# One expert phase of a hybrid encoder layer: rows moved between halves of a turn, a coefficient tile released earlier, and part of a split moved from GpSimd to VectorE

## The reference, cut to what matters

```python
u = jnp.take(u_tab, ib, axis=0)                     # 128 rows of 2048 for each token
h = jax.nn.gelu(jnp.einsum('nkd,nd->nk', u, xb), approximate=False)
vv = jnp.take(v_tab, ib, axis=0)
return jnp.einsum('nk,nkd->nd', gb * h, vv)
```

## Time and profile before

| what | us |
|---|---|
| median of 3 runs | 4788.26 (4786.75 to 4789.27) |
| the profiled execution | 4788.95 |
| its span in the trace | 4787.2 |
| PE busy | 4449.2 (93%) |
| DVE busy | 2972.1 (62%) |
| POOL busy | 2434.3 (51%) |
| ACT busy | 1360.4 (28%) |

### The profile page before, as it was taken

One profiled execution on the slowest core, in us unless ns is written; L12 is line 12 of the kernel. 1 busy time (PEld: TensorE's weight loads), 2 busy tenths in 40 slices (PEclk: granted clock), 3 DMA queues, 4 the chain that ended last, 5 costly groups with the idle time before them and its releaser, 6 DMA issues. The chain is left out here.

```text
span 4787.2 us, 86830 instructions
## 1 busy us (share of the span) xinstructions
PE 4449.2 (93%) x33921; PEld 4303.0 (90%) x33921; DVE 2972.1 (62%) x4301; ACT 1360.4 (28%) x1786; POOL 2434.3 (51%) x929
## 2 busy tenths in 40 slices
PE   6999989999999898979999989999999999999997
PEld 5999888888888798969999989999999999999997
DVE  4333255555555432239996946666787887777786
ACT  3333322222222221122223433332223223233222
POOL 1322222222212133324443347787898998888885
PEclk8999999999999999989999999999999999999998
DMA  6999833444343467853334478888898889888884
GB/s 233 355 360 371 294 126 121 135 136 136 127 136 132 136 221 248 299 196 107 102 114 155 188 270 283 281 286 313 326 333 324 329 322 330 311 306 323 307 297 168
DMA packets 357708, 1141.22 MB, mean 238 GB/s; under 512 B 35089, under 2 KB 128657, under 8 KB 270225
## 3 DMA queue, kind: packets, MB, share of 16 engines
q1 hardware_dynamic: 294400, 780.38, 47.0%
q0 software_dynamic: 46080, 335.56, 18.8%
q10 hardware_dynamic: 17040, 22.58, 1.3%
HBM read 942.00 MB, written 195.32 MB: 238 GB/s over the span
## 5 line engine op out<-in xcount | busy, mean ns | idle before, releaser
L154 POOL TENSOR_TENSOR wlo<-raw,whi 128x2048 fp32r<-128x2048 f32 x174 | 804.1, 4621 | 1981.9 <-ACT whi L150 1686.0
L168 POOL TENSOR_TENSOR wlo<-raw,whi 128x1024 fp32r<-128x1024 f32 x424 | 1067.2, 2526 | 262.0 <-ACT whi L164 258.1
L164 ACT ACTIVATE whi<-raw 128x1024 fp32r<-128x1024 f32 x424 | 448.6, 1059 | 1067.5 <-PE psS L236 553.2
L236 PE MATMUL accs<-xh,whi 128*128 128x272 f32 x2624 | 580.8, 303 | 56.4 <-POOL wlo L154 26.3
L236 PE MATMUL psS<-hh,whi 128*128 128x384 f32 x1600 | 556.2, 348 | 57.1 <-DVE H L2270 52.4
L236 PE MATMUL accs<-xh,wlo 128*128 128x272 f32 x2624 | 546.7, 290 | 0.0
L236 PE MATMUL accs<-xl,whi 128*128 128x272 f32 x2624 | 545.7, 290 | 0.0
L2295 DVE SCALAR_TENSOR_TENSOR H<-R,HD,H 128x2048 f32<-128x2048 f32 x127 | 528.6, 4162 | 0.1
L236 PE MATMUL accs<-hh,whi 128*128 128x272 f32 (+1 forms) x1696 | 459.4, 320 | 49.0 <-POOL wlo L154 24.5
L236 PEld LDWEIGHTS accs<-xh,whi 128*128 128x128 f32 x2624 | 415.9, 190 | 86.9 <-issue 39.3
L236 PE MATMUL psS<-hl,whi 128*128 128x384 f32 x1344 | 465.3, 346 | 0.0
(11 more groups left out here) (424 smaller groups left out, 8973.6 us busy)
## 6 DMA issues: line engine op xcount, KB each, us to landing
raw<-in_u SPq DMA_DIRECT2D x128, 1024.0 KB, 4.9
raw<-in_v SPq DMA_DIRECT2D x128, 1024.0 KB, 5.3
raw<-in_w_in SPq DMA_DIRECT2D x82, 1024.0 KB, 8.1
at_UI<-in_u SPq DMA_DIRECT2D x64, 1024.0 KB, 9.4
u_d<-at_UO SPq DMA_DIRECT2D x256, 256.0 KB, 6.6
wo_UI<-in_u SPq DMA_DIRECT2D x24, 1024.0 KB, 8.9
u_d<-wo_UO SPq DMA_DIRECT2D x96, 256.0 KB, 4.8
g_d<-STG SPq DMA_DIRECT2D x8, 3072.0 KB, 9.7
```

Source lines behind the costliest of these rows:

```text
L154: pool.tensor_tensor(self.lo[:, c % 2, :], self.raw[:, c % 2, :], self.hi[:, c % 2, :].bitcast(F32), ALU.subtract).then_inc(self.split_don ...
L164: act.activation(self.half(self.hi, c, h), self.half(self.raw, c, h), ACT.Copy).then_inc(self.hi_done, 1)
L168: pool.tensor_tensor(self.half(self.lo, c, h), self.half(self.raw, c, h), self.half(self.hi, c, h).bitcast(F32), ALU.subtract).then_inc(se ...
L236: mm = pe.matmul(out, w(k), x(k, n), start=a, stop=z)
```

## The change

It does three things, and adjusts the order around them.

- The rows of a turn: `places` now has 9 of a turn's 13 rows in units 0 to 3. DVE runs `rows(2)`, `rows(2)` at the start of the u half, then as before, so 10 rows stand ahead of the adds of unit 4 and 3 (4 in long turns) in the v half; none stands ahead of unit 7's adds.
- The second half of wlo of each u unit of a turn is made by DVE (`u_second`, semaphore `u_second`), not by POOL. It waits for POOL's first half and for both halves of whi. SP's loads and TensorE's waits for these units go by the two counts (`second_load`, `second_ready`). The one for unit 0 stands between adds 13 and 14 of the turn before, unit 1's after two rows, those of units 2 and 3 after `coef_lo(0)` and `coef_lo(1)`.
- In the first groups, TensorE's first block of the last channel of the last v unit, the last that reads chi and clo tile 0, signals `ex_free`, and ACT makes chi tile 0 on that; tiles 1 to 3 wait as before.

The four loads of H also share one semaphore.

```diff
+        def second_load(sp, src, i, n):
+            if 2 <= n < 6:
+                sp.wait_ge(S["u_second"], 4 * i + n - 1)
+            else:
+                sp.wait_ge(W.split_done, 12 * i + before_u + (2 * n - 2 if n < 2 else 2 * n - 6))
...
+        def second_ready(pe, i, n, half):
+            if n < 4 and half:
+                pe.wait_ge(S["u_second"], 4 * i + n + 1)
+            else:
+                pe.wait_ge(W.split_done, 12 * i + before_u + (n + 1 if n < 4 else 2 * n - 4 + half + 1))
+
+        def u_second(dve, c):
+            dve.wait_ge(W.split_done, 12 * ((c - C0) // U) + before_u + (c - C0) % U + 1)
+            dve.wait_ge(W.hi_done, 2 * (W.base + c) + 2)
+            dve.tensor_tensor(W.half(W.lo, c, 1), W.half(W.raw, c, 1), W.half(W.hi, c, 1).bitcast(F32),
+                              ALU.subtract).then_inc(S["u_second"], 1)
...
-                    W.split_lo_half(pool, c, h)
+                    if c < C0 or (c - C0) % U >= 4 or h == 0:
+                        W.split_lo_half(pool, c, h)
...
-                    done(channel(c, dd, [*range(4)]), dd)
+                    if h == 3 and dd == 3 and per == 4:
+                        channel(c, dd, [0]).then_inc(S["ex_free"], 1)
+                        done(channel(c, dd, [1, 2, 3]), dd)
...
-                        W.wait_used(act, c)
                         for k in range(4):
+                            if k == 0:
+                                act.wait_ge(S["ex_free"], s + 1)
+                            else:
+                                W.wait_used(act, c)
                             coef_hi(4 * s + 4 + k)
...
-                rows(3 if kinds[s] == "long" else 2)
+                c = C0 + U * (s - FIRST)
+                rows(2)
+                u_second(dve, c + 1)
+                rows(2)
                 for k in range(2):
                     scale(4 * s + k)
                     rows(1)
                     coef_lo(4 * s + k)
+                    u_second(dve, c + 2 + k)
                     rows(1)
...
                         if dd == 2:
-                            rows(1)
+                            rows(1 if h == 1 or kinds[s] == "long" else 0)
                         add(s, 4 * h + dd)
-                rows(1)
                 for dd in range(4):
                     add(s, 12 + dd)
+                    if dd == 1:
+                        u_second(dve, c + U)
```

More of the change, by code:

```diff
@@ L1935, in experts @@
                   "last": [(0, 0.1), (0, 0.5), (1, 0.3), (1, 0.7), (2, 0.3), (2, 0.7), (3, 0.3)],
[L1936 to L1939, removed]
+                  "short": [(0, 0.1), (0, 0.4), (0, 0.7), (1, 0.0), (1, 0.3), (1, 0.7), (2, 0.3), (2, 0.6), (3, 0.3),
+                            (4, 0.3), (5, 0.1), (5, 0.7), (6, 0.2)],
+                  "long": [(0, 0.1), (0, 0.4), (0, 0.7), (1, 0.0), (1, 0.3), (1, 0.7), (2, 0.3), (2, 0.6), (3, 0.3),
+                           (4, 0.3), (5, 0.1), (5, 0.7), (6, 0.2), (6, 0.7)]}
         dotted = summed = 0
@@ L1956, in experts @@
         issue = [max(3.0, when[n - GBUF] + 0.4 if n >= GBUF else 0.0) for n in range(len(gathers))]
+        before_u = 2 * (W.base + C0) + 4
+        def second_load(sp, src, i, n):
[3 more added lines that the diff above has]
+                sp.wait_ge(W.split_done, 12 * i + before_u + (2 * n - 2 if n < 2 else 2 * n - 6))
+            raw = W.raw[:, n % 2, :]
+            if len(src.shape) == 3:
+                raw = raw.rearrange("p (k n) -> p k n", k=src.shape[1])
+            sp.dma_start(raw, src).then_inc(W.loaded[n % 2], 16)
+        def second_ready(pe, i, n, half):
[8 more added lines that the diff above has]
+                              ALU.subtract).then_inc(S["u_second"], 1)
         def gates_stored(eng):
@@ L2011, in groups @@
                 for k in range(4):
-                    W.load(sp, row(A["u"], 4 * s + k), C0 + k, U, i)
+                    second_load(sp, row(A["u"], 4 * s + k), i, k)
                 for h in range(4):
-                    v_unit(C0 + 4 + h, i, s, h, U)
+                    src = v_units[s, h] if isinstance(s, int) else v_units[bass.ds(s, 1), h].rearrange("g p k n -> (g p) k n")
+                    second_load(sp, src, i, 4 + h)
                 if not last:
@@ L2058, in u_products @@
                 for h in range(2):
-                    W.ready(pe, c, per, i, h)
+                    if per == U:
+                        second_ready(pe, i, c - C0, h)
+                    else:
+                        W.ready(pe, c, per, i, h)
                     for mm in product(pe, [out], lambda k: W.hi[:, c % 2, k * P:(k + 1) * P], lambda k: W.lo[:, c % 2, k * P:(k + 1) * P],
@@ L2078, in v_first @@
                 for half in range(2):
-                    W.ready(pe, c, per, i, half)
+                    if per == U:
+                        second_ready(pe, i, c - C0, half)
+                    else:
+                        W.ready(pe, c, per, i, half)
                 for k in range(4):
@@ L2096, in v_products @@
                 for dd in range(4):
-                    if dd % 2 == 0:
+                    if dd % 2 == 0 and per == U:
+                        second_ready(pe, i, c - C0, dd // 2)
+                    elif dd % 2 == 0:
                         W.ready(pe, c, per, i, dd // 2)
                     pe.wait_ge(S["ex_added"], 16 * s + 4 * h + dd + 1)
-                    done(channel(c, dd, [*range(4)]), dd)
+                    if h == 3 and dd == 3 and per == 4:
+                        channel(c, dd, [0]).then_inc(S["ex_free"], 1)
+                        done(channel(c, dd, [1, 2, 3]), dd)
+                    else:
+                        done(channel(c, dd, [*range(4)]), dd)
             def v_units_of(c, i, s, per):
@@ L2159, in _ @@
             for q in range(4):
-                act.dma_start(H[:, 4 * q:4 * q + 4, 0:TD], load_h(4 * q, 4 * q + 4)[:, :, 0:TD]).then_inc(S[f"ex_h{q}"], 16)
+                act.dma_start(H[:, 4 * q:4 * q + 4, 0:TD], load_h(4 * q, 4 * q + 4)[:, :, 0:TD]).then_inc(S["ex_h"], 16)
             act.wait_ge(S["ex_cst"], 16)
@@ L2263, in add @@
                 h, dd = d // 4, d % 4
-                if s == 0 and dd == 0:
-                    dve.wait_ge(S[f"ex_h{h}"], 16)
+                if s == 0 and d == 0:
+                    dve.wait_ge(S["ex_h"], 64)
                 if dd % 2:
@@ L2314, in _ @@
                     add(s, 4 * h + 3)
+                    if h == 3 and not ahead:
+                        u_second(dve, C0)
                     if h == 1 and ahead:
@@ L2336, in _ @@
                         if dd == 2:
-                            rows(1)
+                            rows(1 if h == 1 or kinds[s] == "long" else 0)
                         add(s, 4 * h + dd)
-                rows(1)
                 for dd in range(4):
                     add(s, 12 + dd)
+                    if dd == 1:
+                        u_second(dve, c + U)
             s = SUPERS - 1
-            rows(2)
+            c = C0 + U * (s - FIRST)
+            rows(1)
+            u_second(dve, c + 1)
+            rows(1)
             for k in range(3):
@@ L2347, in _ @@
                 coef_lo(4 * s + k)
+                if k < 2:
+                    u_second(dve, c + 2 + k)
                 rows(1 if k < 2 else 0)
```

## The result

The changed kernel takes 4838.1 us (median, 4828.8 to 4840.2) beside 4788.7 for the kernel before: ratio 1.0095, interval 1.0079 to 1.0111. It is slower by 49 us where 76 us less were forecast. Its profiled execution took 4828.82 us (span 4827.0), 39.9 more than the profiled one before.

What follows compares the result with a forecast made beforehand. TensorE was taken as the bound, losing time to waits and clock. Turns 62 + first groups 10.6 + odd turns 5 + 0.5 + 0 - 2 = 76 us less, giving 4712 us; range 4680 to 4775.

Steps and rivals of the forecast that it cites:

- What bounds the kernel, and the floor: Supers 13 to 29: TensorE is the bound; a turn's floor is 67.2 us against 72.9 measured before.
- The rows: Turn's end: with the rows moved, waits of 3.5 and 0.4 us a turn go, and the clock's loss with them.
- some 1 us to spare: End of long turns: despite a second row at unit 6, adds 12 and 13 end in time by this margin.
- `u_second`: DVE's second half of wlo for u units: 1.2 us alone, 2.4 on the mean, upper bound 6.0.
- VectorE as the bound: Rival, u half: DVE stands still for POOL, turns take 77 us, kernel slower at 4849; chance of slower 0.10.
- it lands in 5.1 to 7 us: Unit 4's weight load in each turn: time from issue, at 17.3 us, to landing.
- The walk to unit 4: u half, step by step: POOL's second half ends at about 35, wanted at 33.6; new wait 1.5 us, bounds 0 and 5.
- The clock's loss: Turns of supers 13 to 29: 1.5 to 2 us a turn at a lower clock after long idle time, to go.
- POOL's relief is worth nothing: POOL's four halves less, 9.6 us a turn, win no time: TensorE waits only 9.9 us for it in all.
- DMA becomes the bound: Rival, turns: share 0.96 at 69 us, landings near 12 us, about 4742; chance 0.28, shared with new waits of some 3 us.
- Part 3: Ends of first groups: earlier chi tile 0 wins 8.6 us for nine and 2 for the first, together 10.6, bounds 5 and 20.
- The odd turns: Super 12 wins 5 us, super 11 0.5, super 30 0 (either way 4), super 31 loses 2.

Runs made afterwards that it cites:

- the rows alone: The kernel before with only the changed kernel's moved rows and places, POOL still making both halves of every wlo: 0.9964, 4773.0 us.
- part 3 alone: The kernel before with only chi tile 0 released by its last reader in the first groups: 0.9991, 4788.6 us.
- gathers held: The changed kernel, with POOL holding the seventh gather of a turn until u_second of unit 2 is made: 1.0049, 4823.3 us.

## Why the prediction was wrong, point by point

**What bounds the kernel, and the floor: right.** TensorE bound the turns before and after, and a turn without a stall is near 67.3: the turn from 4435.5 took 68.7 with 1.4 us of wait.

**The rows: right in short turns, too light in long ones.** In short turns from 4026 us on no wait for adds stands at a turn's end. In long ones "some 1 us to spare" was wrong. The end of one in the kernel after, DVE, POOL, PE:

```profile
3499.53 4.55 DVE L2337 SCALAR_TENSOR_TENSOR H<-R,HD,H 128x2048 f32<-128x2048 f32 x1
...
3505.87 3.79 DVE L1980 TENSOR_TENSOR wlo<-raw,whi 128x1024 fp32r<-128x1024 f32 x1
3509.58 1.01 DVE L2312 TENSOR_TENSOR H<-psS,H 128x384 f32<-128x384 f32 x2
...
3506.17 2.40 POOL L168 TENSOR_TENSOR wlo<-raw,whi 128x1024 fp32r<-128x1024 f32 x1
...
3504.60 0.44 PE L236 MATMUL psS<-chi,whi 128*128 128x384 f32 x1 [0.95 <-DVE H L2312]
...
3510.26 0.44 PE L236 MATMUL psS<-hh,whi 128*128 128x384 f32 x1 [1.20 <-DVE H L2312]
```

`u_second` of the next unit 0 stands still for POOL's half and runs into the two last adds; I had written this case down at 0.7 us and put it in a margin. The nine long turns of the stretch wait 2.2 us each for adds (19.9 in all), over half of the 3.9 that were to go.

**`u_second`: right, on the dear side.** I took 2.4 us as its mean between 1.2 and 6.0. It was at its lower bound, 1.2, in 70 of 84 cases (min, median and greatest, in ns):

```profile
L1980 DVE TENSOR_TENSOR wlo<-raw,whi x84: 1205/1215/3949, 3202.8 to 4746.0; 128x1024 fp32r<-128x1024 f32 x84
```

DVE's waits for gelu fell from 264.1 to 113.5 us (3200 to 4760), as foreseen. The rule of the shared port that the Trainium skill states (page "SBUF — State Buffer", section "SBUF: two separate sides") holds where the two meet, 3.79 us against 1.21, but they met rarely. The rival built on it, VectorE as the bound, had the right sign and the wrong mechanism: PE waited 0.6 us for `clo` in all, and with the rows alone the kernel was faster.

**The step that failed: "it lands in 5.1 to 7 us".** The walk to unit 4 was right in each step but this one, and it was the one I took unchanged from the kernel before. The load was issued at 15.8 us into the turn, 1.5 earlier than walked, but took 13.4 us and landed at 29.2 where the walk had 22.4 to 24.3. The new wait at unit 4, priced at 1.5 us with bounds of 0 and 5, measured 5.7 on the mean of the 17 turns.

The sum in its terms: the 17 turns were forecast at 17 x 69.2 = 1176.4 us and took 1297.3, 120.9 more. The waits at unit 4 are 97.4 us in this stretch in place of 17 x 1.5, so 72 more. The waits for adds, 19.9 in place of none, are 20. The rest, 29, is the clock and small gaps: PE was busy for 1179.9 us, 37.5 over 17 x 67.2, where I had put 0.5 a turn. The granted clock fell after all of the waits at unit 4 but the one of 1.4 us, with matmuls 0.32 us apart in place of 0.175, as it did before at ends of turns; from 4544.2 on the granted clock was 0.62 for 4 us, then 1.00 again:

```profile
4544.20:4548.20 4.00, 3.96 (x15) 3.96 (x16) 4.00 (x1) 0.00 (x0) 3.84 (x2) 0.62 0.93 306
```

The clock's loss was to go with the waits; it moved with them instead. I had the number that should have warned me in the same row, the greatest landing of 12.4 us, and used it for a rival only.

**"POOL's relief is worth nothing" was worse than nothing.** I had costed the removed halves at zero because PE hardly waited for POOL. But in the long turns they stood between gathers and spaced them out by 3.5 us. The four halves taken away, with the moved row that frees its buffer early, put five gathers around one load; with either of the parts alone the load lands in 7 to 8 us there. In the short turns, which are the ones I walked, POOL's relief isn't needed for it: the two moved rows alone bring the load to 13.3 us. The walk priced these rows as work of DVE, and not as gathers that are issued earlier.

**The rival "DMA becomes the bound" asked the right question of the wrong number.** It named landings near 12 us and a wait at unit 4, as it came, but it took the mean share of a turn, found 0.96 and priced that at 3 us. The mean share even fell, to 0.83. What counts is the share in the 12 us of one load, 1.01 at 413 GB/s.

**Part 3: right mechanism, half the size.** Nine gaps of the first groups lost 14.1 us before and lose 9.5 now: 4.6 where 8.6 were forecast. One of them, ACT, DVE, POOL, PE:

```profile
2924.63 0.53 ACT L2205 ACTIVATE chi<-GE 128x384 fp32r<-128x384 f32 x1 [1.48 <-PE psS L236]
...
2925.19 2.64 DVE L2302 TENSOR_TENSOR clo<-GE,chi 128x384 fp32r<-128x384 f32 x3 [0.52 <-ACT chi L2205]
...
2921.72 4.74 POOL L168 TENSOR_TENSOR wlo<-raw,whi 128x1024 fp32r<-128x1024 f32 x2
...
2927.13 0.41 PE L236 MATMUL psR<-chi,whi 128*128 128x384 f32 x1 [0.97 <-DVE clo L2302]
```

Chi is ready early, clo is issued at 2925.19 and stands still until POOL's pair ends at 2926.46, as I had said. In seven of the nine POOL ends so late, 0.66 us before the matmul: five of these won 0.4 us and two nothing, and only two ends won 1.3; I had taken half of them for early. The 2 us for the first end didn't come in the changed kernel (7.16 to 6.99), though with part 3 alone 2.8 did.

**The odd turns.** Super 12 won 5.9 (5 forecast), super 30 won 4.0 (0, either way 4), and behind it 5.6 were won where 2 were to be lost. Super 11 lost 6.6 (0.5 to win): unit 4's load took 15.5 us there. Why super 31 won, and some 5 us were won outside the ends of groups ahead of super 11, stays open.

## What to carry to other kernels

A landing time read from the old trace holds only as long as the traffic around the load does: ask of every instruction that is removed from a queue that issues DMAs what it had been spacing out, and of every consumer moved forward what it now frees. Judge DMA by its share in the few microseconds of the transfer that somebody waits for, not by the mean of a turn. If such a load is late, try longer runs per partition for that one load: here this took 1.7% off the changed kernel, issuing it earlier 1.0% and holding gathers back 0.5%. And move one thing at a time: one row moved gave 0.9879, two gave 0.9964, and all three parts 1.0095.

## What the runs showed of the hardware

- A load of 1 MB in runs of 2 KB took mostly 5 us beside spaced gathers (before) and mostly 11 to 16 us among gathers of 8 KB rows that kept the engines at 410 GB/s (changed); in runs of 8 KB among the same gathers it took 7.5 to 10. Gathers issued 0.6 us and more behind it did not delay it (5.1 us, gathers held).
- 410 to 413 GB/s was moved while the load was late, and 0 GB/s in the 4 us from 4536.4 on.
- DVE's operation on two SBUF inputs of 1024 columns takes 1.21 us alone and 3.79 across one half of POOL; POOL's gather instruction takes 0.94 us alone and 2.83 while a v row of DVE, which has two inputs in SBUF too, is running (4537.59, with the row from 4535.83 on). It then ended 0.83 us after the row, whenever it had started.
